# A ring of 20 weight slots instead of 18 for the mixture of experts, its first pair's products by turns, its first and last panel pair by rows

## The reference, cut to what matters

```python
h = h + merged @ w_out[l]
h = h + expert_choice_ffn(rmsnorm_2(h, norm_ffn[l]), w_router[l], w_exp_gate[l], w_exp_up[l], w_exp_down[l])
ple_gate = jax.nn.sigmoid(rmsnorm_2(h, norm_ple[l]) @ w_ple_gate[l])
h = h + ple_gate * (p[l] @ w_ple[l])
return rmsnorm_2(h, norm_final)
...
def expert_choice_ffn(xn, w_router, w_gate, w_up, w_down):
    aff = jax.nn.softmax(jnp.einsum('bsd,de->bse', xn, w_router), axis=-1)
    top_aff, top_idx = lax.top_k(jnp.swapaxes(aff, 1, 2), cap)          # cap = 64
    xg = xn[bidx, top_idx]
    hid = silu(einsum('becd,edf->becf', xg, w_gate)) * einsum('becd,edf->becf', xg, w_up)
    y = einsum('becf,efd->becd', hid, w_down) * top_aff[..., None]
    return jnp.zeros((B, S, D)).at[bidx, top_idx].add(y)
```

## Time and profile before

| what | value |
|---|---|
| median of 3 runs | 1964.71 us |
| the profiled execution's own time | 1965.61 us |
| its span | 1963.9 us |
| granted TensorE clock, mean | 0.997 |
| TensorE busy | 1893.1 us, 96% |
| GpSimd busy | 994.7 us, 51% |
| VectorE, ScalarE busy | 787.9 and 553.8 us |
| first and last load of expert weights issued | 1392.2 and about 1872 us |
| last expert product ends | about 1901.7 us |

### The profile page before, as it was taken

How to read it: one execution, slowest core, us unless ns; L and a number is a source line. 1 busy time by engine, 2 the same in 40 slices (tenths; PEclk the granted TensorE clock), 3 DMA queues, 4 the chain that set the end, 5 groups by cost and what they waited for, 6 DMA issues and landing times.

```text
span 1963.9 us, 23242 instructions
## 1 busy us (share of the span) xinstructions
PE 1893.1 (96%) x9430; PEld 1386.6 (71%) x9430; DVE 787.9 (40%) x1187; ACT 553.8 (28%) x1122; POOL 994.7 (51%) x565
## 2 busy tenths in 40 slices
PE   7999998999999999999999999999999999989988
PEld 6888886688788888888777678887854444433446
DVE  2456668551423301323566375654241222211234
ACT  4535547332422201211133433342230000000025
POOL 5697867667277878887565496546600000000022
PEclk9999999999999999999999999999999999999999
DMA  5321123312123223322322222122989999999981
GB/s 185 97 76 43 44 67 127 108 65 97 44 86 97 96 97 96 97 97 91 114 76 65 65 77 85 54 64 76 347 322 419 421 421 422 421 421 421 421 357 61
DMA packets 92698, 335.81 MB, mean 171 GB/s; under 512 B 7697, under 2 KB 9489, under 8 KB 67761
## 3 DMA queue, kind: packets, MB, share of 16 engines
q1 hardware_dynamic: 89008, 321.82, 44.3%
q10 hardware_dynamic: 3584, 12.52, 1.7%
HBM read 328.01 MB, written 6.29 MB: 170 GB/s over the span
## 4 chain that ended last, share of the span: by engine, by line
PE 83%; DMA 7%; POOL 4%; DVE 3%; ACT 2%; issue 1%; SPq 0%; ACTq 0%; DVEq 0%; POOLq 0%
PE bank L618 51%; PE bank L1889 11%; PE bank L1919 3%; DMA arena<-in_w_exp_up 3%; DMA shared<-in_w_exp_up 3%; PE bank L795 2%; DMA shared<-in_w_exp_down 1%; PE bank L1906 1%; PE bank L639 1%; POOL shared_r L657 1%; POOL shared_r L658 1%; PE bank L1080 1%; POOL shared_r L676 1%; PE bank L1463 1%; PE bank L2028 1%
## 5 line engine op out<-in xcount | busy, mean ns | idle before, releaser
L618 PE MATMUL bank<-shared_r 128*128 128x512 f32 (+1 forms) x3840 | 885.5, 387 | 16.8 <-POOL shared_r L676 7.2
L618 PEld LDWEIGHTS bank<-shared_r 128*128 128x128 f32 x3840 | 693.1, 188 | 170.4 <-issue 15.3
L657 POOL TENSOR_TENSOR shared_r<-shared,small 128x1024 fp32r<-128x1024 f32 (+1 forms) x168 | 327.9, 1952 | 347.3 <-PE bank L618 338.2
L658 POOL TENSOR_TENSOR shared_r<-shared,shared_r 128x1024 fp32r<-128x1024 f32 (+1 forms) x168 | 414.8, 2469 | 13.2
L657 POOL TENSOR_TENSOR spare_r<-arena,small 128x1024 fp32r<-128x1024 f32 x2 | 3.8, 1890 | 483.3 <-DMA arena<-in_w_ple_gate 483.3
L618 PE MATMUL bank<-shared_r,arena_r 128*128 128x512 f32 x768 | 176.1, 391 | 0.0
L618 PEld LDWEIGHTS bank<-shared_r,arena_r 128*128 128x128 f32 x768 | 144.2, 188 | 31.5
L1889 PE MATMUL bank<-arena 128*64 128x512 f32 x688 | 153.0, 594 | 10.9 <-DMA arena<-in_w_exp_up 9.7
L1889 PE MATMUL bank<-shared,arena 128*64 128x512 f32 x672 | 148.0, 593 | 8.2 <-DMA shared<-in_w_exp_up 7.8
L676 POOL TENSOR_TENSOR shared_r<-shared,shared_r 128x1024 fp32r<-128x1024 f32 x40 | 102.4, 2561 | 75.7 <-ACT shared_r L667 75.7
L1889 PEld LDWEIGHTS bank<-arena 128*64 128x64 f32 x688 | 49.2, 137 | 107.6 <-issue 92.3
(11 more groups left out here) (436 smaller groups left out, 2254.7 us busy)
## 6 DMA issues: line engine op xcount, KB each, us to landing
shared<-in_w_in SPq DMA_DIRECT2D x80, 512.0 KB, 3.6
shared<-in_w_exp_up SPq DMA_DIRECT2D x34, 1024.0 KB, 24.4
arena<-in_w_exp_down SPq DMA_DIRECT2D x34, 1024.0 KB, 25.8
arena<-in_w_exp_gate SPq DMA_DIRECT2D x28, 1024.0 KB, 26.0
shared<-in_w_exp_gate SPq DMA_DIRECT2D x26, 1024.0 KB, 26.1
arena<-in_w_exp_up SPq DMA_DIRECT2D x24, 1024.0 KB, 25.9
shared<-in_w_exp_down SPq DMA_DIRECT2D x24, 1024.0 KB, 25.8
shared<-in_w_up SPq DMA_DIRECT2D x32, 512.0 KB, 3.7
```

Of the source, the lines that this page charges most:

```text
L618: ins = pe.matmul(dst, W_, x_, start=first, stop=final)
L657: link(pool.tensor_tensor(hi, raw(p), small[:, 18:19].to_broadcast([P, hi.shape[1]]), ALU.add))
L658: pool.tensor_tensor(lo, raw(p), hi.bitcast(F32), ALU.subtract).then_inc(S_("w_split"), 1)
```

## The change

Four things. (1) The ring gets two slots: `masks`, one tensor that now holds `chunk_mask`, `levels_m`, `band` and `rope`, becomes slot 8, and the upper half of `bc` with `ones` and `tri` behind it (`rows[:, D:D + XPANEL]`) becomes slot 19. The guards move with the numbers, and slot 19 waits for the first gathered bank, since `ones` and `tri` are read until then. (2) `norm_final_2` is no longer loaded before the router: SP loads it into the lower half of `bc`, when the transposes of the last pair are written, ahead of the first parts of `w_ple_gate`. (3) In the first pair the gather's first half is made as two quarters in two banks, and g and u go by turns (g c0 c1, u c0 c1, gather, g c2 c3, u c2 c3); the loads have this order too. The first pair's y takes the next pair's second gather half between its units 1 and 2. (4) The first and the last unit are loaded by rows: one slot holds row block kk = 0 of both experts, the other kk = 1, with a semaphore each.

```diff
-RING = 18
+RING = 20
...
+    masks = sb("masks", [P, XPANEL])
+    chunk_mask = masks[:, 0:4 * CW]
...
+    rows = sb("rows", [P, D + XPANEL])
+    bc = rows[:, 0:2 * D]
+    ones = rows[:, 2 * D:2 * D + S]
...
-    ring = spares + inner[0:6] + outer[4:8] + outer[2:4] + outer[0:2] + inner[6:8]
+    ring = spares + inner[0:6] + [masks[:, :]] + outer[4:8] + outer[2:4] + outer[0:2] + inner[6:8] + [rows[:, D:D + XPANEL]]
...
+    x_order = [("x", 0, "a"), ("x", 0, "b"), ("g", 0, 0), ("g", 0, 1), ("u", 0, 0), ("u", 0, 1), ("x", 0, 1), ("o", 0, 0),
+               ("x", 1, 0), ("t", 0, 0), ("t", 0, 1), ("y", 0, 0), ("y", 0, 1), ("x", 1, 1), ("o", 1, 0)]
...
+    x_units = [(0, w, c) for w, c in ((0, 0), (0, 1), (1, 0), (1, 1), (0, 2), (0, 3), (1, 2), (1, 3))]
+    x_units += [(0, 2, c) for c in range(4)] + [(i, w, c) for i in range(1, PAIRS) for w in range(3) for c in range(4)]
+    by_rows = (0, len(x_units) - 1)
...
+        if n in by_rows:
+            src = src[0, 2 * i:2 * i + 2].rearrange("e (p c r) n -> c r p e n", c=4, r=2)[c, q % 2]
+            sp.dma_start(ring[q % RING].rearrange("p (e n) -> p e n", e=2), src).then_inc(rows_full[q % 2], 16)
...
+                if n in by_rows:
+                    pe.wait_ge(rows_full[kk], 16 * by_rows.index(n) + 16)
...
+                if n in by_rows and kk == 0:
+                    ins.then_inc(S_("x_used"), 1)
...
         if i == 0:
-            expert_gather(pe, 0, 0)
+            expert_gather(pe, 0, "a")
+            expert_gather(pe, 0, "b")
             expert_product(pe, "g", 0, 0, range(0, 2))
+            expert_product(pe, "u", 1, 0, range(0, 2))
             expert_gather(pe, 0, 1)
             expert_product(pe, "g", 0, 0, range(2, 4))
+            expert_product(pe, "u", 1, 0, range(2, 4))
...
-        act.dma_start(bc[:, D:2 * D], A["norm_final_2"].partition_broadcast(P)).then_inc(S_("gain_in"), 16)
...
-            if q == 8:
+            if q == 9:
                 sp.wait_ge(S_("w_split"), parts[late - 1]["split"])
-            if q == 10:
+            if q == 11:
                 bank_written(sp, out2[7])
-            if q == 14:
+            if q == 15:
                 bank_done(sp, BASE["router"])
-            if q == 16:
+            if q == 17:
                 bank_written(sp, ple[7])
+            if q == 19:
+                bank_written(sp, x_bank["x", 0, "a"])
             expert_load(sp, q)
+        bank_written(sp, x_bank["t", PAIRS - 1, 1])
+        sp.dma_start(bc[:, 0:D], A["norm_final_2"].partition_broadcast(P)).then_inc(S_("bc_in"), 16)
         slots_over(sp, 0)
-        slots_over(sp, 16)
+        slots_over(sp, 17)
+        slots_over(sp, 18)
```

## The result

The changed kernel takes 1951.72 us, median of 4 runs (1950.55 to 1953.06), beside 1965.18 us (1960.56 to 1965.83) of the kernel before on the same chip: a ratio of 0.9938 with a 95% interval of 0.9927 to 0.995. It is first laid out by stage, in the two profiled executions (1965.61 and 1951.76 us).

The account below looks back on a forecast made before the run. The experts' weight stream, saturating the DMA engines at 421 to 422 GB/s, was taken as the bound. Terms of -2.5, -3.5 and -0.6 summed to -6.6 us, giving 1958.1 us, range 1954.5 to 1963.5.

Parts of the forecast that it names:

- Slot 8: Load of `masks` moved early, while SP waits for the last split of `w_out`, filling that DMA gap: -2.5 us.
- Slot 19 and the first pair's order: Earlier load and earlier slot releases in the first pair leave no DMA gap from 1457 on: -3.5 us.
- the three gaps: DMA idle time between 1457 and 1474, losing 1.1, 1.6 and 0.9 us, all expected to close.
- The empty stretch: Sign in the DMA windows: 7 us without transfers at 1439 would still be there after the change.
- Sum of both: Gains in the expert weights' stream from the early `masks` load (-2.5) and the first pair's changes (-3.5).
- By rows: At the last down unit, half can run before its last load lands; TensorE's own path limits this to -0.6 us.
- 4 KB rows: Loads by rows read 4 KB HBM rows, not 8 KB; possible cost 0 to 0.5 us, taken as 0.
- The late parts: `norm_final_2` and `w_ple_gate` loads at SP's end land 1.25 us later, hidden by 3.7 us of slack: 0; rival slowdown, chance 0.05.
- The slot alone: Rival: the `masks` load gives its 2.5 us but the gaps behind 1457 stay: 1962.2 us; chance 0.13.
- TensorE as the bound: Rival: TensorE's own path sets the expert stage's end, so an earlier stream is hidden: 1964.7 us; chance 0.08.
- More at both ends: Rival: the row split counts in full and the profile's pace is slow: -7.7 to -9, 1956.5 us; chance 0.16.

Follow-up runs that it names:

- no_rows: The changed kernel with no unit loaded by rows (`by_rows` empty); 1953.36 us, ratio 0.9951 to the kernel before.

## Why the prediction was wrong, and where it was right

**The step that failed** is the sentence "All its bytes must move at a rate that doesn't change; the time can only come from the engines' idle time before they are saturated, and from what lies behind the last landing." It was applied to the whole kernel: the start of the stream was held where it was, and the front was no term of the sum at all. The front is 1.39 ms long and not bound by the stream (43 to 185 GB/s up to slice 28), and there the edit of `ARENA`, which stands in the diff, sped up 1056 matmuls. The first expert load went out 5.6 us sooner. Of these, 3.5 us are the matmuls by their steps (4.1 by their groups). Taking the 64 bytes back gave 3.2 us back to the front (1389.80, in an execution with a different count of half-clock stretches, below), and adding them to the kernel before took 3.1 off (1389.06).

Another 1.6 us came before the first of these matmuls had run (it starts at 667.26 before and at 665.58 after). TensorE enters a run of six matmuls at 343.41 before and 343.21 after, 0.2 us apart, and the next such run 1.8 us apart:
```profile
347.84 1.94 PE L618 MATMUL bank<-shared_r 128*128 128x512 f32 x6
...
346.02 1.95 PE L621 MATMUL bank<-shared_r 128*128 128x512 f32 x6
```
In between, the same window has 8 matmuls at half the granted clock before, and 13 at full clock after:
```profile
343.80:347.20 3.40, 3.40 (x8) 2.23 (x7) 0.63 (x3) 2.15 (x4) 3.32 (x2) 0.50 1.01 405
...
343.80:347.20 3.40, 3.40 (x13) 2.13 (x12) 1.73 (x6) 2.52 (x6) 3.32 (x2) 1.00 0.97 384
```
The changed kernel has its half-clock stretch at 307.8, ahead of waits for GpSimd (1.34 us before, 0.64 after, at 320) that take most of it up. No run shows what moved the stretch. I take it for luck, not for a gain of the change. The 0.5 us of the 5.6 that are left stay untraced. Of the 0.8 us behind the last down unit, 0.6 are the same thing (L621 and L642, step 0.2333 to 0.2267, 95 steps). So some 4 of the 12 to 13.5 us are matmuls that got faster by their operands' distance, 1.6 are the place of a half-clock stretch, and 7.5 are the stage, forecast with 6.6. The part of the sentence on the rate was true of this change, 421 both times, but only because neither layout had the ring aligned.

**Slot 8, -2.5:** the load went out where forecast, and the window of the first 29.4 us gained 0.44 MB, and 0.96 with the 0.52 of `norm_final_2` that left it: nearly a slot. But its own worth, with the rest of the change in place, was 0.6 by the stage. I had counted a gap as lost for good, while further idle time lay behind it in the same stage.

**Slot 19 and the first pair's order, -3.5:** the three gaps are gone, as the windows show, and the two slots together are worth 3.9 us. The credit for the order was wrong; it gave 0.1 beside 20 slots. The empty stretch that I expected to stay at 1439 did stay, moved with the front: 29 GB/s before, 26 after from 1433.4 to 1440.4, and the second of the three windows has 293 and 297.

**Sum of both, -6.0:** the last up unit starts 6.9 us sooner after the gather. Without the longer wait in the kernel before, if that is chance, it is 6.0. The total was right, with its terms wrong among themselves, since they share the same idle time.

**By rows, -0.6:** from the last up unit to the last down quarter it is 19.76 before and 19.16 after, -0.6 exactly; no_rows gives 0.9. TensorE's own path was close behind, as said.

**4 KB rows, 0:** nothing shows. The window of 29.4 us, which begins with the two loads by rows, has 411 GB/s, and the same window of no_rows:
```profile
1386.00:1415.40 29.40, 29.40 (x144) 24.68 (x143) 5.96 (x9) 7.74 (x18) 17.10 (x8) 1.00 1.02 413
```
That is 0.06 MB or 0.1 us. The cost of 0 stands, with the Trainium skill's threshold of 512 B (DMA: Bandwidth & Descriptors, the table at its head) not contradicted here.

**The late parts, 0:** right. GpSimd's first split, to be read against the earlier trace rows:
```profile
1888.84 1.89 POOL L660 TENSOR_TENSOR spare_r<-arena,small 128x1024 fp32r<-128x1024 f32 x1 [478.23 <-DMA arena<-in_w_ple_gate]
```
It is done at 1893.2 with both halves, and the product starts at 1896.22: 3.0 us of slack, where I had counted 3.7.

**The rivals.** The slot alone, and TensorE as the bound, each lost: the gaps closed and the stage shrank. "More at both ends" had the right sign, by a different way. None of the rivals had a term outside the stage.

## What to carry to other kernels

When a diff changes the size of any on-chip tensor, list what moves with it, and compare the matmuls' mean time per group before and after in stages that the change doesn't touch: 64 bytes were worth nearly as much here (3.5 us by the steps) as two slots of buffer (3.9). Place tensors that meet in a matmul at a distance that is a multiple of 256 bytes, and buffers that take a saturated stream at multiples of 256: for the ring it took 128 bytes ahead of `arena` and a `small` packed by 8 columns, and gave another 4.7 us. Savings that fill the same idle time don't add up; count what was moved by the end of the last gap, and not gap by gap.

## What the runs showed of the hardware

- **Matmuls and addresses.** A 128x128 by 128x512 matmul in the split form steps by 0.2269 us where the tensors of moving and stationary tile start a multiple of 256 bytes apart, by 0.2333 (0.2290 with the operands' roles exchanged) at 64 bytes more, by 0.2325 (0.2322) at 128 more. These values repeat to 0.0002 us between kernels with the same distance. No run shows why.
- **DMA and addresses.** 8 KB packets into slots at multiples of 256 bytes take 309 ns, into others (64 and 128 bytes past one) 312 to 313; the stream runs at 427 against 421 GB/s. The Trainium skill (DMA: Bandwidth & Descriptors, the note on 436 against 360) puts the fabric's ceiling at 435 GB/s; the trace agrees so far that both rates stay below it, and says nothing of what sets it. The same note says that about 358 GB/s on the HBM side bind a transfer from HBM to SBUF; here the trace does not agree, with one core at work it was 421 to 427.
- **The clock.** In every execution there are two to four stretches in which the granted clock is at half, the last one at its end. In the changed kernel, two windows of 3 us:
```profile
1328.00:1331.00 3.00, 0.89 (x4) 0.39 (x3) 3.00 (x2) 0.00 (x0) 2.92 (x2) 1.00 0.16 58
1332.00:1335.00 3.00, 3.00 (x16) 3.00 (x16) 1.28 (x2) 1.77 (x3) 0.00 (x0) 0.50 0.51 175
```
TensorE had been busy for 0.89 of 3 us, and when it takes up work the granted clock is at 0.50, the 1.2 GHz level. Their number and place before the experts differ from kernel to kernel; what moves them isn't shown. The fronts show what they cost: with two of them and the fast distance 1385.7 to 1387.0 (nine kernels), with three 1387.3 and 1389.1. And with two in either kernel the place alone was worth 1.6 us, as told above. So a front can't be compared to less than 2 us from one profile each.
